# Dealing the pieces of the input projection evenly over the channel tiles of a scan

## The reference, cut to what matters

```python
h = rms_norm(x, mix_norm_g)
proj = h @ w_in                       # 2048 -> 8192 columns
q, k, v, u, gate_a, gate_b = split(proj)   # 2048, 512, 512, 1024, 2048, 2048
...                                   # attention uses q, k, v, later
lam_bar = exp(lam * step)             # complex, 64 groups x 64 states, two directions
bu = einsum('bsgc,gnc->bsgn', u, b_bar)
_, states = associative_scan(_ssm_combine, (a, bu), reverse=reverse, axis=1)
y = real(einsum('bsgn,gcn->bsgc', states, c_mat))
y_ssm = y_fwd + y_bwd + ssm_d * u
y_act = gelu(y_ssm)                   # goes into the gated unit
y_b = (y_act @ glu_w_a) * sigmoid(y_act @ glu_w_b)
merged = sigmoid(gate_a) * y_a + sigmoid(gate_b) * y_b
```

## Time and profile before

| | us |
|---|---|
| Median of three runs | 4194.48 (4186.1 to 4198.58) |
| The profiled execution, its own time | 4178.98 |
| its span | 4177.3 |
| First turn of tile 0 (line 782) starts | 82.02 |
| c(3) of the tiles 0 to 7 starts | 148.47, 226.12, 302.51, 379.98, 456.18, 533.53, 612.86, 681.88 |
| First matmul of the gated unit starts | 689.01 |

### The profile page before, as it was taken

How to read it: one execution, slowest core, us unless ns; L and a number is a source line. 1 busy time by engine, 2 the same in 40 slices (tenths; PEclk the granted TensorE clock), 3 DMA queues, 4 the chain that set the end, 5 groups by cost and what they waited for, 6 DMA issues and landing times. The chain is left out here.

```text
span 4177.3 us, 41165 instructions
## 1 busy us (share of the span) xinstructions
PE 3361.3 (80%) x13955; PEld 1710.2 (41%) x13955; DVE 2428.8 (58%) x4303; ACT 766.6 (18%) x1832; POOL 1633.2 (39%) x1133
## 2 busy tenths in 40 slices
PE   8989967999896888555888889988878885568787
PEld 6333433444584555211222238555745551112222
DVE  3777766520158777877554522421687788765553
ACT  1000002310110110575000011231110107740000
POOL 0000000000025656687666600000256667877674
PEclk9999988999998989766899989969989996679998
DMA  6333321234358999899999963403589999999998
GB/s 216 115 118 108 121 73 67 101 122 139 121 188 311 354 380 380 315 351 355 372 377 392 385 237 128 151 30 121 208 323 365 367 356 324 346 335 383 376 376 325
DMA packets 317003, 1066.62 MB, mean 255 GB/s; under 512 B 95634, under 2 KB 104674, under 8 KB 215906
## 3 DMA queue, kind: packets, MB, share of 16 engines
q0 software_dynamic: 147456, 717.84, 45.1%
q1 hardware_dynamic: 134240, 335.05, 22.5%
q10 hardware_dynamic: 35120, 11.33, 1.1%
HBM read 1417.99 MB, written 2.10 MB: 340 GB/s over the span
## 5 line engine op out<-in xcount | busy, mean ns | idle before, releaser
L2002 DVE CUSTOM_DVE_ANT_0 sc<-big,hs 128x2048 f32<-128x2048 f32 x512 | 1174.6, 2294 | 653.6 <-DMA big<-in_peer_down,sc 312.0
L698 PE MATMUL bank<-wring,ht 128*128 128x512 f32 (+1 forms) x1792 | 800.3, 605 | 2.4 <-ACT ht L1234 1.7
L1066 PE MATMUL bank<-big,sc 128*32 128x512 f32 x4096 | 647.5, 716 | 103.8 <-DVE sc L2021 51.4
L1005 PE MATMUL bank<-wring 128*128 128x512 f32 x1024 | 535.0, 658 | 101.1 <-DMA wring<-in_dense_up 80.1
L698 PEld LDWEIGHTS bank<-wring,ht 128*128 128x128 f32 x1792 | 346.1, 196 | 426.8 <-issue 421.0
L988 PE MATMUL bank<-ht,wring 128*128 128x256 f32 x2048 | 518.2, 405 | 0.2 <-DMA wring<-in_dense_down 0.2
L632 POOL DMA_INDIRECT big<-in_peer_up,sc x256 | 392.9, 1535 | 278.1 <-PE bank L1066 139.5
L632 POOL DMA_INDIRECT big<-in_peer_v,sc x256 | 402.7, 1573 | 247.4 <-PE bank L1066 92.7
L632 POOL DMA_INDIRECT big<-in_peer_down,sc x256 | 408.2, 1595 | 232.6 <-DVE sc L1976 92.6
L632 POOL DMA_INDIRECT big<-in_peer_u,sc x256 | 406.0, 1586 | 226.6 <-DVE sc L1976 92.1
L988 PEld LDWEIGHTS bank<-ht,wring 128*128 128x128 f32 x2048 | 397.5, 201 | 210.6 <-issue 157.1
(11 more groups left out here) (376 smaller groups left out, 2836.1 us busy)
## 6 DMA issues: line engine op xcount, KB each, us to landing
wring<-in_w_in SPq DMA_DIRECT2D x84, 1024.0 KB, 5.5
wring<-in_dense_down SPq DMA_DIRECT2D x64, 1024.0 KB
wring<-in_dense_up SPq DMA_DIRECT2D x256, 256.0 KB
wring<-in_w_out SPq DMA_DIRECT2D x32, 1024.0 KB, 5.0
wring<-in_w_attn_o SPq DMA_DIRECT2D x16, 1024.0 KB, 5.0
wring<-in_peer_w_query SPq DMA_DIRECT2D x16, 1024.0 KB, 4.8
wring<-in_peer_w_q SPq DMA_DIRECT2D x16, 1024.0 KB, 4.8
wring<-in_glu_w_a SPq DMA_DIRECT2D x8, 1024.0 KB, 5.0
```

Of the source, the lines that this page charges most:

```text
L698: mm = pe.matmul(dense_bank[2 * pair + t][:, 0:w_cols], lhs[:, k, t * P:(t + 1) * P], wslot[:, b, kk * w_cols:(kk + 1) * w_cols], start=(k ...
L1005: mm = pe.matmul(dense_out[t][:, :], dense_w[:, r, t * P:(t + 1) * P], sup[:, m % 2, r % 4, :], start=(r == 0), stop=(r == DENSE - 1))
L1066: mm = pe.matmul(acc_bank[j][32 * q:32 * q + 32, :], w_blocks[:, u % 2, g, :], gslot[:, m % RING, q * 512:(q + 1) * 512], start=(u % PH == ...
L2002: v.tensor_tensor_reduce(dot_out, gslot[:, m % RING, :], h[:, u // PH, :], 1.0, 0.0, ALU.mult, ALU.add, sub(rAC)[:, i:i + 1]).then_inc(dot ...
```

## The change

Each of the eight tiles now has seven pieces: tile k does the pieces 7k to 7k + 6 of the 56, counted over all rounds. The table `at` becomes (0, 3, 5, 6, 7): part 0 has pieces 1 and 2, part 1 has 3 and 4, part 2 has piece 5 and part 3 has piece 6. A group of four may now end anywhere in a tile, so ACT has a table `done_after` that says after which step's sines a group that ends with piece i is copied. ACT's loop over the first six tiles is written out; PE's was already. The weights' order on SP, the whole of DVE and of POOL are the same.

```diff
-            def ssm_tile(k, r, slots):
-
-                at = {8: (0, 3, 5, 7, 8), 4: (0, 2, 3, 4, 4)}[len(slots)]
+            def input_slot(r, b):
+                dense_slot(b, R_QKV + r, hT, 2 * (R_QKV + r))
+
+            def ssm_tile(k):
+
+                at = (0, 3, 5, 6, 7)
+                slots = [divmod(7 * k + i, SLOTS) for i in range(7)]
...
-                dense_slot(slots[0], r, hT, r * 2)
+                input_slot(*slots[0])
...
                 for m in range(4):
                     part = slots[max(1, at[m]):at[m + 1]]
-                    for b in part[:-1]:
-                        dense_slot(b, r, hT, r * 2)
+                    for r, b in part[:-1]:
+                        input_slot(r, b)
                     if m < 3:
                         b_times_u(k, m + 1)
-                    for b in part[-1:]:
-                        dense_slot(b, r, hT, r * 2)
+                    for r, b in part[-1:]:
+                        input_slot(r, b)
                     c_times_states(k, m)
 
 
             pe.wait_ge(sp_done, 2)
-            for k in range(SSM_K - 2):
-                ssm_tile(k, k + R_QKV, range(SLOTS))
-
-            ssm_tile(SSM_K - 2, R_GLU - 1, range(4))
-            ssm_tile(SSM_K - 1, R_GLU - 1, range(4, SLOTS))
-
+            for k in range(SSM_K):
+                ssm_tile(k)
...
-            def ssm_tile(k, i, groups):
-
+            def ssm_tile(k):
+
+                done_after = {0: 1, 1: 3, 2: 3, 3: 5, 4: 5, 5: 7, 6: 7}
+                ends = [divmod(7 * k + i, SLOTS) + (done_after[i],) for i in range(7) if (7 * k + i) % 4 == 3]
...
-                    if s in groups:
-                        dense_evac(i + R_QKV, groups[s], proj, (i * 2 + groups[s]) * 512)
+                    for r, b, after in ends:
+                        if after == s:
+                            dense_evac(R_QKV + r, b // 4, proj, (r * 2 + b // 4) * 512)
...
-            with act.Fori(0, SSM_K - 2) as k:
-                ssm_tile(k, k, {5: 0, 7: 1})
-                reload_bc(k)
-            last = R_GLU - 1 - R_QKV
-            ssm_tile(SSM_K - 2, last, {7: 0})
-            reload_bc(SSM_K - 2)
-            ssm_tile(SSM_K - 1, last, {7: 1})
+            for k in range(SSM_K):
+                ssm_tile(k)
+                if k < SSM_K - 1:
+                    reload_bc(k)
```

## The result

The changed kernel takes 4121.8 us (median of four runs, 4113.23 to 4129.35), the kernel before 4193.09 (four runs, 4186.1 to 4198.58). The ratio is 0.983, with a 95% interval from 0.9805 to 0.9855: 61 to 82 us less. The forecast was 4135, a gain of 59.3. Run again beside other kernels it took 4124.43 against 4184.54, ratio 0.9839 (0.9807 to 0.9871), 54 to 81 us less. The profiled execution took 4113.2 and its span is 4111.5.

What follows compares the result with a forecast made beforehand. Bound by DVE's serial eight-step walk in every tile, plus reload waits at six starts. Walk, starts, one exposed start and POOL put tile 7's c(3) at 622.6 against 681.88: 4194.48 - 59.3 = 4135 us, range 4111 to 4160.

Steps and rivals of the forecast that it cites:

- The walk: Inside each tile, DVE's serial steps with PE's bu and c between: 56.19 us from step 0's line 1731 to c(3).
- the stop: PE behind c(1), before bu(3): a new wait of 3.45 us for DVE's line 1732 of step 5.
- The clock behind the stop: After PE's new stop the clock falls: bu(3) to c(2) takes 10.62 us instead of 8.13, adding 2.49.
- rival 1: The clock does not fall at the new stop before bu(3): gain 68 us, time 4126; chance 0.14.
- DVE's wait at step 6: DVE at line 1753 of step 6 must wait for c(2): 1.78 us late.
- The small stops: PE's stops of 1.03 us at bu(1) and 0.8 at c(3): no clock fall, pieces stay at 7.1 us.
- Rival 2: Clock falls after small stops at bu(1) and c(3) too, costing 40 us: time 4175; chance 0.19 including mixtures.
- The reload: B and C at tile starts: hidden at six, c(3) to DVE's step 0 10.13 us against 19.90; tile 4 exposed, +9.77.
- the slack: At six tile starts, B is ready 0.3 to 0.8 us before PE wants it.
- Rival 3: Reload lands late, PE waits at tile starts: about no gain (4194), chance 0.04; slower (4207 and more), chance 0.03.
- POOL beside DVE: POOL's products beside DVE's last steps: 0.2 us added at six starts, 1.2 in all; at worst 1.85 per start.
- The sum: c(3) of tile 7 at 147.35 + 7 x (56.19 + 10.13) + 9.77 + 1.2 = 622.6 us, against 681.88.

Runs made afterwards that it cites:

- the corners: Between the kernel before (scan 599.86 us) and the changed kernel with the reload freed in tile 3 too (scan 531.34 us; 4113.56 us, ratio 0.9822).
- the version with quarters: Changed kernel with reload freed in two halves behind sines of steps 2 and 4, pieces cut into quarters dealt over the whole tile: 4071.95 us, ratio 0.9737.

## Why the prediction was right

**The walk.** It was made of tile 0's own times, and the changed tile 0 has them to a few hundredths: the stop is 3.39 (I had 3.45), the wait at step 4 is 2.15 (2.2). The reading that the short tiles are held by the serial walk of DVE and not by PE's work carried the sum.

**The clock behind the stop.** From bu(3) to c(2) the eight tiles took 11.32, 9.78, 11.47, 9.78, 9.77, 11.47, 9.78 and 11.47 us, mean 10.6; the sum had 10.62 from four rows of tiles 6 and 7. A fall followed all eight stops, so rival 1 is out. I had taken the freely running period of the Trainium skill ("TensorE: Matmul & The Clock Gate", "What's actually happening") as leave for stops without a fall. No run here shows one, only two lengths of fall. In seven of the ten traces there are stops of this length, 44 in all, and every one was followed by a fall: 28 times bu to c took 9.77 to 9.83 us, 16 times 11.32 to 11.48. That the eight of this trace were four and four, like the four that gave the mean, is luck: all long or all short would have moved the sum by 6.8 us. DVE's wait at step 6 follows the length: 2.42 in tile 0, where I had 1.78 for the mean. Tile 0's c(3) was 1.0 us later than forecast, 0.7 by the longer fall and 0.3 in DVE's last steps, which lay beside POOL's products; the short falls of other tiles gave it back. I had written that tiles 6 and 7 of the kernel before stop three times each; with the stop in front of c(3), 7.78 us in the earlier trace rows, it is four.

**The small stops.** 1.03 at bu(1) and 0.73 to 1.02 at c(3) were followed by no fall; the pieces are 7.13 and 7.03. Rival 2 is out.

**The reload.** The heaviest term. c(3) to bu(0) at a free start is 8.88 us, as forecast (10.13 - 1.25), and at the one exposed start, into tile 4, 365.98 - 347.33 = 18.65, the mean I had used. What I had close to wrong is the slack: from the first issue to POOL's first product took 147.59 - 138.61 = 8.98 instead of 7.66, and it still fitted, because c(3) of that tile was late as well: POOL was done at 149.52, PE wanted B at 150.45. At the other free starts it took 8.0 to 8.7, and at two of the three behind a short fall the slack was only 0.2 (at the first of them POOL was done at 214.22 + 1.51 = 215.73, B wanted at 215.94). That all six starts stayed free was in part luck. Rival 3 wanted some 18 us from issue to POOL. The reading that matters, that the copy's table moves the reload, was in the order of ACT's instructions and not in the words of the change; the experiments show it holds 57 to 61 of the 68.5 us between the corners.

**POOL beside DVE.** In the changed kernel the longest line 1757 was 643 ns against a median of 419, so 0.2 us as forecast. Where POOL's products met DVE's scan, in the version with quarters, the step took 0.77 longer. Neither is the full 1.85.

**The sum.** 540.5 forecast, 540.32 measured (538.13 the second time). Against the runs the forecast gain of 59.3 is 12 us short in the first comparison, 2 below the interval's lower end, and nearly exact in the second (60.1 between medians); the scatter of the rest, 21 us between the shortest and longest trace, is larger than that difference. Why the rest scatters stays open.

## What to carry to other kernels

When a change regroups work, look in each queue for what stood behind the regrouped instruction: here eight small DMAs stood behind a copy that waited for the last matmul, and setting them free gave most of a gain that the even deal seemed to explain. Before a stop on TensorE is filled, ask where the time reappears: in these runs a stop and its fall of the clock cost least where another engine's step covered them, and most in front of c(3), with DVE's next step waiting behind. Filler is worth cutting finer than the stops: with pieces of 7.1 us DVE was busy under 90% of a tile in every order tried, with quarters of 1.8 us, and the reload issued earlier, both were busy over 94% of a tile.

## What the runs showed of the hardware that was not expected

- Stops of 3.39 us in front of bu were followed by the 1.2 GHz clock in 44 cases of 44 (four before the change, eight after, the others in five of the experiments), while those of 1.22 and less inside the tiles were not. The fall cost 1.64 to 1.70 or 3.19 to 3.35 us in two clusters, not a spread.
- The fall needn't lie inside the stop. In tile 0 of the changed kernel it does: the granted clock is 0.76 in the last half microsecond before bu(3) and 0.50 from there on. In tile 3 the stop ends at 328.70, bu(3) takes 1.20 us, and the granted clock is 0.82 from 329 to 330 and 0.50 from 330 to 331: it fell when PE had been working again for about a microsecond.
- Four products on POOL took 1.51 to 2.33 us beside DVE's last steps, 2.23 to 2.46 beside its scan, and 1.47 in all but one of the starts before the change, where DVE was waiting for most of that time. DVE lost 0.2 to 0.3 us beside the first (tile 0) and 0.8 beside the second.
